# Two-layer hybrid encoder on one core: attention bodies turned by one weight unit, retention unrolled, first loads reordered

## The reference

```python
h = rmsnorm(x, norm1_g)
q_r, k_r, v_r, g_r, q_d, k_d, v_d, ga, gb = split(h @ w_in)
# retention, 4 heads: rotate q_r, k_r; decayed scores; o_r, S_new
# differential attention, 8 heads: q_d, k_d = rope(rmsnorm(.)); a = p0 - lam * p1; o_d = a @ v
y = sigmoid(ga) * (rmsnorm(o_r) * silu(g_r) @ w_branch_a) + sigmoid(gb) * (rmsnorm(o_d) * (1 - lam0) @ w_branch_b)
x = x + y @ w_out
u = rmsnorm(x, norm2_g) @ w_up
x = x + (silu(conv(u)_g) * conv(u)_a) @ w_down      # conv over 3 rows
```

## Time and profile before

| what | value |
|---|---|
| median of 3 runs | 2384.08 us (2383.68 to 2388.91) |
| the profiled execution | 2388.49 us |
| its span, first to last instruction | 2386.6 us |
| mean granted TensorE clock | 0.993 |
| DMA | 193.28 MB, 81 GB/s over the span |

### The profile page before, as it was taken

The page is one execution under the profiler, slowest core; times in us unless marked ns, Lnnn a source line. Parts: engine busy times, 40 slices in busy tenths (PEclk is TensorE's granted clock), DMA queues, the critical chain, the costliest instruction groups (busy, mean ns, idle before and its releaser), DMA issues.

```text
span 2386.6 us, 50229 instructions
## 1 busy us (share of the span) xinstructions
PE 2297.6 (96%) x17560; PEld 2188.9 (92%) x17560; DVE 1131.4 (47%) x1918; ACT 966.5 (40%) x1829; POOL 851.3 (36%) x380
## 2 busy tenths in 40 slices
PE   5999999999999999999999999999999999999999
PEld 5788889889999999999988898798999999999999
DVE  3644453333545576156344644533345455742663
ACT  3544553333423343244335545533343234422443
POOL 3243232223433343343451342232333443434433
PEclk9999999999999999999999999999999999999999
DMA  4132212121222222322232122122122222223223
GB/s 150 51 102 70 85 60 68 60 90 60 89 72 89 83 88 70 108 89 73 80 99 72 63 83 85 51 83 86 60 72 75 72 89 89 84 75 101 90 67 105
DMA packets 81237, 193.28 MB, mean 81 GB/s; under 512 B 7232, under 2 KB 36000, under 8 KB 81056
## 3 DMA queue, kind: packets, MB, share of 16 engines
q1 hardware_dynamic: 59120, 172.38, 22.0%
q10 hardware_dynamic: 21936, 18.56, 2.4%
HBM read 177.50 MB, written 13.42 MB: 80 GB/s over the span
## 4 chain that ended last, share of the span: by engine, by line
issue 57%; PE 25%; POOL 14%; DVE 2%; ACT 1%; POOLq 0%; DVEq 0%; ACTq 0%
POOL wlo L490 11%; PE ps L602 6%; PE ps L604 6%; PE ps L603 6%; POOL rstd L496 3%; PE ps L961 2%; PE ps L962 2%; PE ps L963 2%; DVE ca L1943 1%; PE ps L641 0%; PE ps L642 0%; PE ps L643 0%; PE ps L669 0%; DVE af L1957 0%; DVE odif L1828 0%
## 5 line engine op out<-in xcount | busy, mean ns | idle before, releaser
L490 POOL TENSOR_TENSOR wlo<-raw,whi 128x1024 fp32r<-128x1024 f32 (+1 forms) x330 | 758.7, 2320 | 1338.4 <-ACT whi L1007 1338.4
L602 PE MATMUL ps<-hl,whi 128*128 128x272 f32 x2496 | 723.6, 290 | 2.4 <-DVE hl L1847 2.4
L604 PE MATMUL ps<-hl,wlo 128*128 128x272 f32 x2496 | 719.6, 288 | 0.0
L603 PE MATMUL ps<-hl,whi 128*128 128x272 f32 x2496 | 718.2, 288 | 0.0
L602 PEld LDWEIGHTS ps<-hl,whi 128*128 128x128 f32 x2496 | 471.6, 189 | 4.3 <-issue 2.8
L604 PEld LDWEIGHTS ps<-hl,wlo 128*128 128x128 f32 x2496 | 470.1, 188 | 0.0
L603 PEld LDWEIGHTS ps<-hl,whi 128*128 128x128 f32 x2496 | 469.7, 188 | 0.0
L641 PE MATMUL ps<-whi,hl 128*128 128x256 f32 x1536 | 446.6, 291 | 11.7 <-ACT rk L1234 10.2
L642 PE MATMUL ps<-wlo,hl 128*128 128x256 f32 x1536 | 438.9, 286 | 0.0
L643 PE MATMUL ps<-whi,hl 128*128 128x256 f32 x1536 | 438.1, 285 | 0.0
L1007 ACT ACTIVATE whi<-raw 128x1024 fp32r<-128x1024 f32 (+1 forms) x330 | 313.2, 996 | 224.0 <-PE ps L963 177.2
(11 more groups left out here) (214 smaller groups left out, 2926.5 us busy)
## 6 DMA issues: line engine op xcount, KB each, us to landing
raw<-in_w_units_dram SPq DMA_DIRECT2D x266, 512.0 KB, 4.7
raw<-in_w_down_units_dram SPq DMA_DIRECT2D x64, 352.0 KB, 3.3
out_new_k_prompt_dram<-rawk ACTq DMA_DIRECT2D x8, 512.0 KB, 3.0
out_new_v_prompt_dram<-vd ACTq DMA_DIRECT2D x8, 512.0 KB, 3.0
x<-in_x_dram ACTq DMA_DIRECT2D x8, 272.0 KB, 11.4
out_y_dram<-x SPq DMA_DIRECT2D x8, 272.0 KB, 5.7
kc_n<-in_cache_k_dram SPq DMA_DIRECT2D x8, 256.0 KB, 2.9
vc_n<-in_cache_v_dram SPq DMA_DIRECT2D x8, 256.0 KB, 3.3
```

The source lines that it names most:

```text
L490: ins = e.tensor_tensor(wlo[:, s, a:b], raw[:, s, a:b], whi[:, s, a:b].bitcast(F32), ALU.subtract)
L602: e.matmul(out, wh, hi, start=(c == 0), stop=False)
L603: e.matmul(out, wh, lo, start=False, stop=False)
L604: ins = e.matmul(out, wl, hi, start=False, stop=(c == KC - 1))
```

## The change

The q unit of the first two heads is made in S, chunk by chunk into five banks (`S_BANKS`), before the statistics. The body D is now k, v, gate and the q of the next body (after the last, the q and k of the first retention head). Gate and next q are filler, in chunks: 16 before the transposes of k, then 5 in each of ten steps, the rest before the last values. R is one body with four heads and 11 units; the scalings of `oret` are spread over the next head's evictions. All units shift by one: unit 1 of D was k and is v, unit 2 was v and is the gate, and so on. POOL's program for D stays. The sample sum of k goes behind the rotation of q.

At the start the loads of x are split over two queues with the first weights between them, the parameters are loaded in two parts, all chunks are rounded first and squared later, and the statistics use one matmul per block, since the last squares are added too. The order of the weights in memory follows. The diff, cut to its core:

```diff
-ORDER = [("S", 1), ("D", 4), ("R", 2), ("M", 1), ("F", 1), ("G", 1)]
+ORDER = [("S", 1), ("D", 4), ("R", 1), ("M", 1), ("F", 1), ("G", 1)]
...
+        S_BANKS = ("t", "o", "s0", "s1", "s0b")
...
-            return (j + (phase == "G")) % 2
+            return (j + (phase in ("D", "R", "G"))) % 2
...
+            for c in range(0, KC, 2):
+                e.dma_start(x[:, c, :], A["x"][c]).then_inc(*S.up(f"x_in{c}", "x", n=16))
+                if c < 4:
+                    a = c * UNIT // 4
+                    e.dma_start(raw[:, 0, a:a + UNIT // 2], A["w_first"][0, :, a:a + UNIT // 2]).then_inc(*S.up(f"first{c // 2}", "in", n=16))
...
@@ pool_program
                 with S.body("S"):
-                    norm_power("s0")
-
                     for s in ("mm_ready", "act_step", "dve_step", "cs_out"):
...
+                    lo("S", 1)
+                    norm_power("s1b")
                 with S.body("D") as p:
                     lo("D", 1)
                     lo("D", 2)
...
                     lo("D", 3)
                     power(20, "k")
                     lo("D", 4)
...
@@ pe_program
-            e.wait_ge(*S.at("tables", "in"))
...
-                    stats("s0")
+                    e.wait_ge(*S.at("w_ready", k=0))
+                    for m in range(TILES):
+                        acquire(S_BANKS[m], act=1, dve=int(m == NT))
+                    for c in range(KC):
+                        for m in range(NT):
...
+                    stats("s1b")
...
+                    n_unit(0, hl1, xs)
...
-                    n_unit(2, hl1, xs, after=queries)
+                    n_unit(1, hl1, xs, after=queries)
                     cached_keys(0)
-                    e.wait_ge(*S.at("w_ready", k=3))
-                    t_tile(3, 0, 0, hl1, act=1)
...
+                            if c == 0:
+                                filled[1] = mm_bank()
+                                acquire(filled[1], act=1, dve=int(kind == "s"))
...
+                    fill(FILL_FIRST)
...
-                        gate_chunks(GATE_SHARE[n])
+                        fill(FILL_SHARE[n])
...
+                    fill(len(FILL) - filled[0])
                     values(9)
...
+        FILL_FIRST = 16
+        FILL_SHARE = (5, 5, 5, 5, 5, 5, 5, 5, 5, 5)
...
@@ act_program
             for c, part in CUT:
                 e.wait_ge(*S.at(f"x_in{c}", "x"))
-                norm_chunk(c, part, vecs[:, 0, c:c + 1])
-                if c in (3, 5):
-                    e.wait_ge(*S.at("raw0", k=32))
+                norm_hi(c, part, vecs[:, 0, c:c + 1])
+                if c in (2, 4):
                     hi("P", 0, c // 2 - 1)
+            for c, part in CUT:
+                norm_square(c, part)
...
+                    square(rawq, "q")
                     prev = None
                     t = 0
-                    for u, (name, buf) in enumerate((("q", rawq), ("k", rawk), ("v", vd))):
+                    for u, (name, buf) in enumerate((("k", rawk), ("v", vd))):
...
+                    hi("D", 3, 0)
+                    hi("D", 3, 1)
                     e.wait_ge(*S.at("t_ready", ("kc", 0)))
...
+                                if tt == 3:
+                                    hi("D", 4, 0)
+                                    hi("D", 4, 1)
...
+                                if u == 0 and m:
+                                    scale_ret(hh - 1, m - 1)
...
@@ dve_program
-                    sample_sum(rawq[0:DEC, NT, :], "mm0", ("N", 0, 4), "q")
                     qk_sums("q")
-                    qk_apply(rawq, "q", 0, lambda: sample_sum(rawk[0:DEC, NT, :], "mm1", ("N", 1, 4), "k"))
+                    qk_apply(rawq, "q", 0)
+                    sample_sum(rawk[0:DEC, NT, :], "mm0", ("N", 0, 4), "k")
                     qk_sums("k")
...
                     qk_apply(rawk, "k", 1)
-                    sample_sum(vd[0:DEC, NT, :], "mm0", ("N", 2, 4), "v")
+                    sample_sum(vd[0:DEC, NT, :], "mm1", ("N", 1, 4), "v")
```

More of the change, by code:

```diff
@@ L533, in pool_program @@
                     lo("D", 4)
[L534 to L539 removed]
+                with S.body("R"):
+                    for j in range(1, UNITS["R"] + 1):
+                        lo("R", j)
+                        if j % 3 == 2:
+                            h = j // 3
+                            e.wait_ge(*S.at("dve_step", ("ms", "ret", h)))
+                            e.tensor_tensor(rsr[:, :], msr[:, :], mhalf[:, 0:TILES], ALU.pow).then_inc(*S.up("pool_step", ("rstd", "ret", h)))
                 with S.body("M"):
@@ L614, in stats @@
                 for m, a, b in blocks:
-                    for n, t in enumerate((acc[:, a:b], sq[:, 1, a:b])):
-                        ins = e.matmul(pv(bank, b - a, 1, m), t, one[:, :], start=(n == 0), stop=(n == 1))
+                    ins = e.matmul(pv(bank, b - a, 1, m), acc[:, a:b], one[:, :], start=True, stop=True)
                 ins.then_inc(*S.up("st_ready", "stats"))
@@ L986, in program, with filled_at @@
         SOFF = [0, 512, 896, 1152]
-        GATE_SHARE = (3, 2, 2, 2, 1, 2, 2, 2, 4, 4)
-        GATE_AT = [next(n for n in range(10) if sum(GATE_SHARE[:n + 1]) >= KC * t) for t in (1, 2, 3)]
+        FILL = ([("g", t, c) for t in range(4) for c in range(KC)] + [("q", t, c) for t in range(NT) for c in range(KC)]
+                + [("s", 0, c) for c in range(KC)])
+        FILL_FIRST = 16
+        FILL_SHARE = (5, 5, 5, 5, 5, 5, 5, 5, 5, 5)
+        FILL_DONE = {}
+        for end in range(KC, len(FILL) + 1, KC):
+            kind, t, _ = FILL[end - 1]
+            FILL_DONE[(kind, t)] = ([-1] if end <= FILL_FIRST else []) + [
+                n for n in range(10) if FILL_FIRST + sum(FILL_SHARE[:n + 1]) >= end] + [10]
+        def filled_at(n):
+            return [tile for tile, at in FILL_DONE.items() if at[0] == n]
         def act_program(S):
@@ L1020, in rest_copy, with norm_hi, norm_square @@
                     *S.up(f"act_free_{bank}", ("rest",) + key))
-            def norm_chunk(c, part, g):
+            def norm_hi(c, part, g):
+                h = span(part)
+                S.settle()
+                e.activation(hl1[:, c, 0, h], x[:, c, h], ACT.Copy, scale=g).then_inc(*S.up("h_hi", ("hi", c, part)))
+            def norm_square(c, part):
                 h = span(part)
@@ L1517, in dve_program @@
             e.memset(ssr[:, :, :], 1.0).then_inc(*S.up("dve_step", key="ones"))
-            e.wait_ge(*S.at("params", "in"))
+            e.wait_ge(*S.at("gains", "in"))
             for c, part in CUT:
                 norm_lo(c, part, vecs[:, 0, c:c + 1])
-                if 0 < c < KC - 1:
-                    norm_sum(c)
+            for c, part in CUT:
+                if c and part != 0:
+                    norm_sum(c, part)
             e.wait_ge(*S.at("lambdas", "in"))
```

402 lines of the change are left out of this document (228 added, 174 removed).

## The result

| what | before | after |
|---|---|---|
| median | 2385.27 us of 4 runs (2383.68 to 2388.91) | 2573.16 us of 4 runs (2571.94 to 2575.16) |
| the profiled execution | 2388.49 us | 2573.29 us |
| its span | 2386.6 us | 2571.5 us |
| mean granted TensorE clock | 0.993 | 0.954 |

The changed kernel takes 1.0786 times as long, with an interval of 1.0772 to 1.0801. The profiled executions differ by 184.8 us; the forecast was 191.7.

A forecast was written before the change was run, and what follows sets the result against it. It took PE's matmuls plus PE's pauses as the bound. +212 + 42 - 17.3 - 8.5 - 7.6 - 11.9 - 13 - 4 = +191.7 us on 2388.5 gave 2580, or 2576 against the median; stated 2578 us, range 2530 to 2618.

The forecast's parts named there:

- The two waits: Per attention body, PE waits for DVE's sample sums of k (13.6 us) and v (12.9 us); +212 us over eight bodies.
- 9.5 us: Sign to look for: POOL's q power right after its second low half, about 9.5 us into the v unit.
- The clock: PE at half rate after the sixteen new waits, 2.6 us lost each: +42 us, bounds 27 to 82.
- one and a half stretches: Half-rate work assumed after each new wait, in stretches of 3.4 us; 2.6 us lost per wait.
- The removed waits: Gone: query waits 17.3 us, their half-rate stretches 8.5, waits at attention body ends 7.6, retention waits with one stretch 11.9.
- The start: Kernel start: first matmul near 16 us, 16 us gained, about 2.7 us of new waiting; net -13 us (-8 to -18).
- just in time: Kernel start: the k unit's own weights were to be ready at about 33.5 us, when needed.
- The layer boundary: Second layer's start: PE starts at about 1205.7, the half-rate stretch goes, 2.7 us of waiting appear; -4 us.
- (2): Rival: only one of the two new waits is real; 2454 us, chance 0.07.
- (4): Rival: PE stays at half rate far longer after each wait and ACT's queue adds 1 us a body; 2626 us, chance 0.05.
- (3): Rival: POOL reaches the q power before the v unit starts, so only the gains stay; 2326 us, chance 0.08.
- products and rotation 5.3: Step in the 2326 us rival's query chain: DVE's products and rotation take 5.3 us, queries ready about 17 us into the body.

The follow-up runs named there:

- e1: Changed kernel with POOL's q and k powers of the attention body each moved ahead of one low half; 2402.98 us, 1.0079 of before.
- e3: Changed kernel with only POOL's k power moved ahead of low half 3, the q power left behind low half 2; 2459.09 us, 1.0315 of before.
- e5: Changed kernel with unread matmuls added, 100 before the second v tile and 96 before the second gate tile; 2546.15 us, 1.0676 of before.
- e6: e1 with the first loads put back on their old queues and order; 2406.75 us, 1.0095 of before.
- e8: e1 with POOL's clears of nmax and qz in S put behind the low half and the rs power; 2397.77 us, 1.0056 of before.
- e12: e1 plus k sum before q rotation, queries transposed later, q power inside low half 1, clears last, v sum between k products and rotation; 2358.91 us, 0.9897.

## Why the prediction was right, step by step

**The two waits** were +212 in the sum and are 205.3, 13.1 and 12.55 us each instead of 13.6 and 12.9. Their place, their releaser, and the POOL instruction behind them are as forecast, and so is that DVE's rotation has its short form there. POOL's q power begins 61.93 - 55.36 = 6.6 us into the v unit and ends at 10.1. The "9.5 us" of the prediction is neither by its own rows, where the power begins 6.85 us after the unit's start and ends at 10.4; the chain's length wasn't affected. e1 to e3 show the cause by taking it away.

**The clock** was +42 and is 27 (e5) to 33 (the stretches). The term that was mis-sized most is "one and a half stretches" of 3.4 us after each wait; the mean over the sixteen is 4.1 us, 1.2 stretches. The lower bound of the prediction, 27, was nearer. The better row was the stretch after the short wait at 153, and the kernel's start was no guide: in the changed kernel PE is at full rate 4.4 us after its first matmul (18.82 to 23.2), with matmuls of 256 columns from the start. In the kernel before it was 10.2 us, of which the first 4.3 went to twelve statistics matmuls of one column each. Whether these were the reason isn't shown.

**The removed waits:** the queries' 17.3 us and their five half-rate stretches, 8.5, are gone, and so are the 7.6 us at the body's end. The retention stage from its first head to its last took 162.04 us before (418.29 to 580.33) and 156.15 after (513.39 to 669.54); in the second layer, where the half-rate stretch of before lies, 163.57 and 156.15. That is 5.9 + 7.4 = 13.3 us, and 11.9 was forecast.

**The start** was -13 and is -7: the v unit starts at 55.36, its like before at 62.31. The first matmul came at 18.8, not 16. Of DVE's six low parts in the row at 13.26, the two that ran beside POOL's low half took 2.34 and 2.69 us, where the trace of before has 0.78 to 0.79; that is 3.5 us, more than the whole miss. And the k weights were not "just in time" at 33.5 but ready at 39.24, 4.20 us late. This has another reason: POOL's clears, which stand in front, began only at 30.84, after 13.03 us of waiting for DVE's last arithmetic on the lambdas, and that stood behind the late low parts and the sums. The prediction counted POOL's own work and left out what POOL waits for.

**The layer boundary** was -4 and is +3.4: from the last down-projection matmul to the v unit 37.59 us, before 34.24. The 3.1 us wait for ACT's eviction was forecast (2.7). Not forecast were the 3.00 us of idleness without a releaser before the first matmul of the second layer; the prediction had PE start at 1205.7 on the data alone, under 1 us behind the last matmul in front. Nor did the half-rate stretch there go: there are two of 3.4 us, at 1296.36 and 1320.26.

Together: 205.3 + 27 - 17.3 - 8.5 - 7.6 - 13.3 - 7.0 + 3.4 = 182.0, or 188 with the clock at 32.6, and 184.8 were measured. The mechanism was right, and the costs came within a tenth; that the total of 192 is only 7 us off is partly luck, because its errors half cancel (-7, -9 to -15 and -1 against +6 and +7). The lower end of the range adds up to 2525 and not 2530.

**The rivals.** (2), only one wait real, is out by the two rows. (4), a longer half rate, is out by the clock term. (3) is the instructive one. Its mechanism is right: with POOL's powers moved, e1, 170 us go and the kernel is within 1% of before. Its price, 2326, was wrong by 77 us. Two steps of it failed. The deadline was taken as the moment when PE asks for the queries, 19 us into the body, though the prediction had itself found that DVE must free the bank first, at 16.1. And "products and rotation 5.3" held no contention, while POOL's low half, now behind the power, ran straight beside the rotation: +4 us. Together they are the 49.3 us of waiting and, behind it, 36.7 us of work at the half clock, 18 us; the rest of the 77 are the start and the layer boundary. 2340, expected of e1, carried the same two errors.

What stays open: the clock's part between 27 and 33 us; why some waits of about 2.1 us are followed by a half-rate stretch and others of the same length aren't; and what is idle for 3.00 us at the layer boundary. No run takes the overlap of rotation and low half away on purpose, so its price rests on rows of traces. And e6 to e8 rest on differences of 4 to 5 us whose intervals overlap e1's.

## What to carry to other kernels

When a loop is turned by one stage, write down every in-order queue of the body again: an instruction whose inputs are now ready early gains nothing while it stands behind one that is now released late, and it takes everything behind it along. Find the first thing that each chain must deliver (here a bank, freed by a small sum at the chain's end, and wanted one tile, three microseconds, before the data themselves) and place that thing between the steps of the chain, as e12 does, not at the end and not where it blocks the queue. And when a chain moves, look up what it then runs beside.

## What the hardware showed that was not expected

- Behind waits of 13 us PE did no more work at the lower clock than behind shorter ones: 2.9 to 5.6 us. After e1's waits of 4.8 to 6.4 us it was 3.4 to 5.3 us. In the kernel before, four of the eight waits of 2.15 us were followed by a stretch, 3.4 us three times and 6.8 us once, and four by none.
- The granted clock in the records reads 1.00 in the first microseconds of PE's work while the matmuls start 0.21 us apart (20 in 4.3 us). There the spacing is the measure. The stretch in after, columns as above:

```profile
18.80:23.10 4.30, 4.28 (x20) 4.29 (x21) 3.72 (x6) 0.69 (x2) 0.00 (x0) 1.00 0.79 244
```

- PE and ACT are at times idle with nothing that they wait for: 3.00 us ahead of the second layer's first matmul, and 1.80 to 1.85 us on ACT at six of the eight body starts, ahead of the square with which the q chain begins.
- DVE and POOL slow one another: rotation steps go from 0.32 to 2.4 us, a product from 1.49 to 3.45 and a low part of the activations from 0.78 to 2.69, and POOL's two low halves from 4.66 to 5.27 and 6.81 us. Each of these DVE instructions loses 1.6 to 2.0 us, the short step as much as the long product, so in these rows the price goes by how many instructions are hit and not by their length.
